# Routed experts in 32-row parts on four column groups of TensorE, in an order made on the chip, with a weight ring of two instead of three

## What is computed

```python
def _swiglu(x, w_gu, w_down):
    g, up = jnp.split(x @ w_gu, 2, axis=-1)
    return (jax.nn.silu(g) * up) @ w_down

def _moe(u, router_w, router_b, exp_w_gu, exp_w_down, shared_w_gu, shared_w_down):
    scores = jax.nn.sigmoid((u @ router_w).astype(jnp.float32))
    _, idx = lax.top_k(scores + router_b.astype(jnp.float32), TOP_K)      # 8 of 128 experts
    s_sel = jnp.take_along_axis(scores, idx, axis=-1)
    wts = s_sel / jnp.sum(s_sel, axis=-1, keepdims=True) * ROUTED_SCALE
    routed = ...   # for each token the weighted sum of _swiglu of its 8 experts
    return routed + _swiglu(u, shared_w_gu, shared_w_down)

# reference(), one layer, 512 tokens of 1024 features, all float32:
#   h = x + g1 * mixer(norm(x))     (a gated recurrence and a gated linear attention)
#   h = h + g2 * moe(norm(h))       out = norm(h)
```

## Time and profile before

| | us |
|---|---|
| runs, median (lowest to highest) | 1280.92 (1279.49 to 1283.02) |
| the profiled execution, its own time | 1282.25 |
| its span | 1280.4 |
| first gate and up product starts | 597.44 |
| last down product ends (starts at 1210.49, runs 3.60) | 1214.09 |
| PE busy over the span | 1216.9 |

### The profile page before, as it was taken

The page is one execution under the profiler, slowest core; times in us unless marked ns, Lnnn a source line. Parts: engine busy times, 40 slices in busy tenths (PEclk is TensorE's granted clock), DMA queues, the critical chain, the costliest instruction groups (busy, mean ns, idle before and its releaser), DMA issues.

```text
span 1280.4 us, 21371 instructions
## 1 busy us (share of the span) xinstructions
PE 1216.9 (95%) x5960; PEld 702.8 (55%) x5961; DVE 603.5 (47%) x1080; ACT 468.4 (37%) x573; POOL 249.4 (19%) x297
## 2 busy tenths in 40 slices
PE   5899999999999999989978999999999999999985
PEld 5678887877888878754323333333343333333332
DVE  4542456659445587763423343423324343234227
ACT  5581225564324232321333334234334343334201
POOL 1000000000000000031433343432434343334200
PEclk9799999999999999989989899999999999999987
DMA  9532203213554674428999996984998989766295
GB/s 335 166 106 82 75 17 115 68 66 132 180 166 145 221 266 154 170 91 318 416 374 369 359 394 260 390 333 152 388 382 305 384 323 390 275 215 255 81 385 239
DMA packets 83842, 305.37 MB, mean 238 GB/s; under 512 B 12627, under 2 KB 15931, under 8 KB 60889
## 3 DMA queue, kind: packets, MB, share of 16 engines
q1 hardware_dynamic: 64120, 261.86, 55.2%
q0 software_dynamic: 14752, 34.48, 7.1%
q10 hardware_dynamic: 4928, 8.49, 1.9%
HBM read 293.92 MB, written 29.89 MB: 253 GB/s over the span
## 4 chain that ended last, share of the span: by engine, by line
PE 82%; DMA 9%; DVE 4%; issue 2%; ACT 2%; SPq 1%; POOL 1%; POOLq 0%; PEld 0%; ACTq 0%; DVEq 0%; PEldq 0%
PE psum L1524 32%; PE psum L1747 23%; PE psum L1794 11%; DMA stage<-in_exp_w_gu 4%; PE psum L1732 3%; PE psum L1497 2%; DMA stage<-in_exp_w_down 2%; PE psum L1817 2%; PE psum L1808 1%; PE psum L1626 1%; DMA xg<-u_rows,row_idx 1%; PE psum L1557 1%; DMA ring<-in_ada_w 1%; PE psum L1671 1%; PE psum L1782 1%
## 5 line engine op out<-in xcount | busy, mean ns | idle before, releaser
L1747 PE MATMUL psum<-w_now,xT 128*64 128x512 f32 x1600 | 362.1, 606 | 16.1 <-DVE w_now L1395 16.0
L1747 PEld LDWEIGHTS psum<-w_now,xT 128*64 128x64 f32 x1600 | 110.3, 140 | 225.7 <-issue 206.8
L1794 PE MATMUL psum<-w_now,mask 128*64 128x512 f32 x784 | 176.4, 592 | 0.0
L671 POOL COPY w_now<-stage 128x2048 f32 x52 | 98.8, 1911 | 252.3 <-issue 209.1
L1524 PE MATMUL psum<-uT_hi,w_hi 128*128 128x512 f32 x352 | 139.3, 396 | 1.1 <-DVE w_lo L444 1.1
L1524 PE MATMUL psum<-uT_hi,w_lo 128*128 128x512 f32 x352 | 137.0, 389 | 0.0
L1524 PE MATMUL psum<-uT_lo,w_hi 128*128 128x512 f32 x352 | 137.0, 389 | 0.0
L444 DVE TENSOR_TENSOR w_lo<-ring,w_hi 128x1024 fp32r<-128x1024 f32 x80 | 94.5, 1221 | 87.1 <-ACT w_hi L437 85.3
L939 ACT ACTIVATE w_now<-stage 128x2048 f32 x52 | 98.7, 1910 | 78.9 <-DMA stage<-in_exp_w_gu 56.7
L437 ACT ACTIVATE w_hi<-ring 128x1024 fp32r<-128x1024 f32 x80 | 82.7, 1056 | 118.0 <-PE psum L1524 59.6
L946 ACT ACTIVATE sel<-psum 128x256 f32<-128x256 f32 x50 | 19.2, 384 | 268.9 <-PE psum L1747 268.9
(11 more groups left out here) (284 smaller groups left out, 1606.2 us busy)
## 6 DMA issues: line engine op xcount, KB each, us to landing
stage<-in_exp_w_gu SPq DMA_DIRECT2D x104, 1024.0 KB, 8.5
stage<-in_exp_w_down SPq DMA_DIRECT2D x52, 1024.0 KB, 8.2
ring<-in_w_in SPq DMA_DIRECT2D x56, 512.0 KB, 5.1
ring<-in_ada_w SPq DMA_DIRECT2D x32, 512.0 KB, 4.7
slots<-expert_rows SPq DMA_DIRECT2D x16, 1024.0 KB, 15.6
ring<-in_ada_w SPq DMA_DIRECT2D x4, 1024.0 KB, 13.3
scale_w<-in_ada_w SPq DMA_DIRECT2D x4, 1024.0 KB, 14.5
ring<-in_w_branch_b SPq DMA_DIRECT2D x8, 512.0 KB, 5.7
```

The source lines that it names most:

```text
L671: pool.tensor_copy(w_now[:, q, 4:6], staged(turn, 4, 2)).then_inc(dn_moved, 1)
L1747: mm = pe.matmul(moe_bank(GU)[at, :], xT[:, s % 2, k, at], gu_part(q, k), start=(k == 0), stop=(k == KT - 1))
L1794: mm = pe.matmul(moe_bank(Y0 + g)[at, :], hT[:, j, at], dn_part(q, j, g), start=(j == 0), stop=(j == 1))
```

## The change

The rows of an expert are cut into parts of 32, and a step handles four parts, one in each group of 32 columns (`STREAMS` = 4). Parts are dealt in turn: part p goes to step p // 4 and stream p % 4. So a large expert sits in all four streams, its consecutive parts side by side, and its weights are copied into up to four places of `w_now`. The experts' order is made on the chip: they are ranked by their count, and taken largest, smallest, second largest, second smallest and so on. `w_now` doubles to four places, and to make room the ring has two places (`STAGES = 6 - STREAMS`), the residual rows are written to DRAM (`h_dram`) ahead of the routed loop and read back (`h_back`) ahead of the tail, and the gathered rows use other buffers. The first weights too now go through the ring; they can be loaded once the order is known. Tables carry two streams per word (`turns_of`).

```diff
-STREAMS = 2
+STREAMS = 4
 W = P // STREAMS
...
-STAGES = 3
+STAGES = 6 - STREAMS
+PAIRS = STREAMS // 2
...
+        def turns_of(eng, n):
+
+            turns = []
+            for j in range(PAIRS):
+                word = eng.value_load(turn_words[0:1, bass.ds(PAIRS * n + j, 1)], min_val=0, max_val=256 * E + E)
+                turns += [word % 256, word // 256]
+            return turns
...
+            for t in range(TT):
+                sp.wait_ge(h_res, TT + t + 1)
+                sp.dma_start(h_dram.rearrange("(t p) d -> p t d", p=P)[:, t], x_tok[:, t]).then_inc(h_out, 16)
+
+            sp.wait_ge(loads_ready, 1)
+            n_loads = sp.value_load(load_count[0:1, 0:1], min_val=TOP_K, max_val=E)
+
+            def load(l, free=None):
+
+                e = sp.value_load(load_expert[0:1, bass.ds(l, 1)], min_val=0, max_val=E - 1)
+                if free is not None:
+                    freed = sp.value_load(load_free[0:1, bass.ds(free, 1)], min_val=1, max_val=TABLE)
                 for g in range(2):
...
+                    if not isinstance(l, int) or l:
+                        sp.wait_ge(gu_in[g], l * 16)
+                    if free is not None:
+                        sp.wait_ge(gu_moved[g], freed)
+                    sp.dma_start(staged(l, 2 * g, 2).rearrange("p a n -> p (a n)"), gu_half(e, g)).then_inc(gu_in[g], 16)
+                if not isinstance(l, int) or l:
+                    sp.wait_ge(dn_in, l * 16)
+                if free is not None:
+                    sp.wait_ge(dn_moved, freed)
+                sp.dma_start(staged(l, 4, 2).rearrange("p a n -> p (a n)"), dn_whole(e)).then_inc(dn_in, 16)
+
+            for l in range(STAGES):
+                load(l)
             sp.wait_ge(tables_ready, 1)
...
+                        with sp.If(n_loads > j + STAGES):
+                            load(j + STAGES, j)
...
+            def move_down(n, qs=range(STREAMS)):
+
+                if not isinstance(n, int) or n:
+                    pool.wait_ge(y_psum, n + 3)
+                turns = turns_of(pool, n)
+                for q in qs:
+                    with pool.If(turns[q] > 0):
+                        pool.wait_ge(dn_in, turns[q] * 16)
+                        pool.tensor_copy(w_now[:, q, 4:6], staged(turns[q] + STAGES - 1, 4, 2)).then_inc(dn_moved, 1)
...
+                turns = turns_of(dve, n)
+                for q in qs:
+                    with dve.If(turns[q] > 0):
+                        dve.wait_ge(gu_in[0], turns[q] * 16)
+                        dve.tensor_copy(w_now[:, q, 0:2], staged(turns[q] + STAGES - 1, 0, 2)).then_inc(gu_moved[0], 1)
...
+            own(stt(key_col, rank_col, -2.0, spare_col, ALU.mult, ALU.add))
+            own.settle()
+            own(stt(key_col, rank_col, 2.0, key_col, ALU.mult, ALU.min))
+            own.settle()
+            ts(load_b, iota_row[:], key_col, 1.0, ALU.subtract, ALU.is_equal).then_inc(key_ready, 1)
+            ts(upto_b, iota_row[:], key_col, 0.0, ALU.subtract, ALU.is_gt).then_inc(key_ready, 1)
...
+            move_first(0, (2, 3))
             shared_up(1)
+            dve.wait_ge(h_out, 16 * TT)
+            move_first(0, (0, 1))
             gated_up(0)
             move_first(1)
...
-            def gate_up(n, s, loads):
+            def gate_up(n, s, copies):
...
-                        pe.wait_ge(gu_moved[g], loads + STAGES)
+                    pe.wait_ge(gu_moved[g], copies)
...
```

More of the change, by code:

```diff
@@ L109, in plan @@
     jobs += [(("out", 1, 3), "dve")] + turned(2) + turned(3)
[L110 removed]
+    jobs += [("router", "act"), ("count", "dve"), ("rank", "dve"), ("loads", "dve"), ("pos", "dve"), ("bstart_col", "dve"), ("bstart_row", "dve"), ("table", "dve")]
     jobs += [(("sgu", m), ("act", "dve")[m % 2]) for m in range(4)]
@@ new lines, in _ @@
+            own.settle()
+            stt(key_row, bank("rank")[:, 0:P], 2.0, spare_row, ALU.mult, ALU.min).then_inc(dve_emptied, 1)
+            wait_emptied(dve, "rank")
+            ts(before_b, key_row, key_col, None, ALU.is_gt).then_inc(order_ready, 1)
+            wait_job(dve, "loads")
+            own(dve.memset(load_expert[:, E:E + STAGES].bitcast(F32), 0.0))
+            own(dve.tensor_copy(load_expert[:, 0:E], bank("loads")[0:1, 0:E]))
+            dve.tensor_copy(load_free, bank("loads")[0:1, E:2 * E]).then_inc(dve_emptied, 1)
@@ L1314, in _ @@
+            own.settle()
+            wait_emptied(dve, "loads")
+            dve.nop().then_inc(loads_ready, 1)
             own(dve.tensor_reduce(w_sum[:], w_left, AX_X, ALU.add))
@@ L1697, in _ @@
             pe.wait_ge(mask_ready, 1)
-            product("count", lambda t: mask_b[:, t], lambda t: ones_b[:, 0:1], dst=bank("count")[:, 0:1], tiles=TT)
+            start_job("count")
+            for t in range(TT):
+                pe.matmul(bank("count")[:, 0:1], mask_b[:, t], ones_b[:, 0:1], start=(t == 0), stop=(t == TT - 1))
+            for t in range(TT):
+                mm = pe.matmul(bank("count")[:, P:2 * P], ones_b[:], mask_b[:, t], start=(t == 0), stop=(t == TT - 1))
+            end_job(mm)
+            pe.wait_ge(less_ready, 1)
+            product("rank", lambda k: ones_b[:], lambda k: less_b, dst=bank("rank")[:, 0:P], tiles=1)
+            shared_product(0, range(5, 6))
+            pe.wait_ge(key_ready, 2)
+            start_job("loads")
+            pe.matmul(bank("loads")[0:1, 0:E], id_cols[:, 0:1], load_b, start=True, stop=True)
+            end_job(pe.matmul(bank("loads")[0:1, E:2 * E], id_cols[:, 2:3], upto_b, start=True, stop=True))
             start_job("pos")
@@ L1787, in _ @@
                 pe.wait_ge(hT_ready, b + 1)
-                pe.wait_ge(dn_moved, loads + STAGES)
+                pe.wait_ge(dn_moved, copies)
                 pe.wait_ge(y_ready, b + 2)
```

284 lines of the change are left out of this document (146 added, 138 removed).

## The result

The changed kernel takes 1496.39 us (median of 4 runs, 1494.56 to 1498.93); the kernel before, beside it, 1281.97 us (4 runs, 1279.49 to 1284.44). The ratio is 1.167, 95% interval 1.165 to 1.170. The profiled execution has a span of 1495.1 us against 1280.4.

A forecast was written before the change was run, and what follows sets the result against it. PE's chain of waits was taken as the bound, with DMA no bound on average. A loop of 787 us against 616.65 (+170), start +9 and tail 0 took 1282.25 to 1460 us, range 1330 to 1575.

The forecast's parts named there:

- ten with two new loads: Loop steps up to 29 where the second load is issued only after the first has landed; 20 us each.
- nine with four copies: Loop steps with four weight copies per engine, one POOL copy ahead of DVE's last; 15.3 us plus 1.9 of clock, 17.2.
- eleven others: Loop steps with three or fewer copies; 12.2 us and 2 for loads and clock, 14.2 each.
- eight rounds: Steps 30 to 34 and 36 to 38, a whole round through the two-place ring between gate and up products; 30.1 us each.
- the early case: Loop steps with two new loads, if they do not wait for loads; 15.3 us.
- the late one: Loop steps with two new loads, if both landings are waited for in turn; 23 us, 26 with the longest landing.
- The rival that bytes or bandwidth set the time: Rival stated for the SP reordering: late steps need more loads than DMA brings, loop within 20 us of 785; no chance given.
- The rival of groups that do not run together: Products take 10.7 us more per step with two column groups at a time; time near 1770 us, chance 0.08.
- Start: Ahead of the first gate and up: two more copies per engine after the last shared product; +9 us, between 4 and 14.
- Tail: Behind the loop: the extra 2 MB written and read back lie beside other work; put at 0.
- The faster rival: Loads in the loop are hidden and only copies count; loop 555 us, kernel 1229 us, chance 0.07.
- The rival of half waits: Loop waits for loads are half those priced, rounds of 22 and two-load steps of 16; time near 1355 us, chance 0.12.

The follow-up runs named there:

- mended order: SP sends a load's down transfer behind the next load's gate and up transfers; changed kernel 1400.68 us, kernel before 1277.4 us, kernel before with two places 1301.69 us.
- quarters: Changed kernel with SP's down transfer behind the next gate and up, each column group walking its own quarter of the list; 1431.34 us, with loop spans of 8 steps 1374.52.
- second dealt run: Changed kernel with SP's down transfer behind the next gate and up, and loop spans of 8 steps in place of 16; 1373.78 us, loop 689.0.
- two kernels with spans of eight: Changed kernel with down transfers behind the next gate and up and 8-step loop spans, once with a list quarter per column group (1374.52 us), once with dealt parts (1373.78).
- with spans of eight: Changed kernel with the loop over steps grouped in spans of 8 instead of 16; 1474.88 us, time behind the loop 67.7 us instead of 89.1.

## Why the prediction held, and where its terms did not

The profiled time was predicted at 1460 us and is 1496.86. The loop was 2 us under its forecast, the start 14.6 and the tail 22.8 over theirs. What the prediction named as its signs is there: 1280 down instructions, 131 copies, 7.07 us for 64 instructions, and in the loop a DMA share of 0.64 and a clock of 0.85.

**The loop: 787 predicted, 785.0 measured.** The classes of steps, taken from the starts of the gate and up products:

| steps | predicted, us each | measured |
|---|---|---|
| ten with two new loads | 20 | 20.2 |
| nine with four copies | 17.2 | 17.0 |
| eleven others | 14.2 | 14.8 |
| eight rounds (30 to 34, 36 to 38) | 30.1 | 28.9 (26.1 to 33.2) |
| last two | 12 | 13.4 |

The eight rounds are where the prediction put them, and step 35, which it left out of them, took 17.7 us. The 20 us of the steps with two new loads is right as a mean only: up to step 12 they take 13.5 to 17.8 us, near the early case (15.3), and after it 21.1 to 25.3, near the late one (23). One of them owes its length to something else. In step 14, 21.1 us under both orders of SP, the chain goes through no landing, but through two stretches in which DVE waits for nothing that the profile shows (the "issue" rows below); the prediction had no such term. That such classes add up to 785 is partly luck.

```profile
816.75 4.27 issue
...
823.40 2.60 issue
```

**Within a round the sum was right and its terms were not.** In the round shown, landing was 5.0 us, not 8.5, and DVE's copy 1.2, not 4.2, since POOL had finished; this is 6.5 less. But POOL made three copies before SP could go on, not 1.5, and they took 6.2 us, not 2.8:

```profile
1222.57 8.03 POOL L703 COPY w_now<-stage 128x2048 f32 x4 [6.88 <-issue]
```

The first of these four ran from 1222.57 to 1225.09, 2.52 us in place of 1.88, as DVE's last copy ran until 1223.34; the third ended at 1228.76. POOL began 1.8 us after the down product, not 1.1 (so in all eight rounds), as it reads two words for the four streams first (line 485); and SP took 2.8 us from POOL's copy to its transfer, not 1.0, as it sends the down transfer and reads two table values in between. Those are 5.9 more. Over the eight rounds POOL made 1.9 copies on average ahead of SP's transfer, and their number orders the rounds: with one copy they took 26.1 to 26.3 us, with two 28.5, with three 28.8 to 32.1; one more, with one copy but a second landing to wait for, took 33.2. So the copies were priced somewhat too low, the table reading on POOL and SP (2.5 us) was left out, and a landing priced 3.5 us too long hid both. The path of the round was right; that its sum was right is luck.

**The cause.** The prediction held that the down transfer's wait for POOL stands ahead of the next expert's weights in one queue. The experiment that changes only this took 102 us of the 168.4 away (95.7 by the medians), all of it from the steps where the prediction has loads waiting. The rival that bytes or bandwidth set the time is refuted with it for this part. The loop in us, under the old and the mended order of SP:

| kernel | old | mended |
|---|---|---|
| before, three places | 616.65 | 610.8 |
| before, two places | 689.1 | 633.9 |
| four groups, quarters | - | 672.3 |
| four groups, dealt (the change) | 785.0 | 682.9 |

The effects do not simply add: the mended order is worth 5.8 us with three places, 55.2 with two, and 102.1 with two and four dealt groups. Down the mended column the ring costs 23.1, four groups 38.4, dealing 10.6 (17 by the second dealt run, 689.0; the medians of the two kernels with spans of eight, 1374.52 and 1373.78, do not differ, as the start comes 7 us later with quarters). 40 steps of more experts each do not run faster than 49 steps of fewer: each gate and up product still waits 3.2 us on average for a copy (with quarters 145.4 us in all, 21.1 of them before the first). How much of the 38.4 is the crowding of new experts and how much the clock, granted at 0.92 against 0.97 over the whole kernel, these runs do not separate. A ring of three under four groups was not tried, since the change gives the third place up for the larger `w_now`.

**Column groups.** Full concurrency was taken from the pair of the earlier trace rows, and the trace confirms it: 7.07 us for 64. The rival of groups that do not run together is out. "TensorE: Matmul & The Clock Gate" of the Trainium skill gives a ratio of 2.38 for three column tiles (Part 3, measured speedup); the loss that it would mean here does not show with four groups in float32.

**Start: +9 predicted, +23.6 measured; this term was mis-sized.** The longer tables moved the shared products' end from 597.4 to 605.0, the 7 us that were priced. Then came 16 us to the first product, where only 2.4 to 3.8 us of copies were expected. 4.8 of them are POOL's copies beside DVE's, by the experiment that moved them. The prediction had this exclusion in its step of four copies and did not apply it to step 0. The others are order on DVE: its first two copies stand behind the index reading and the masks for step 4 (606.13 to 609.56), which wait for PE's last `find`, though PE has nothing left to run then. This last was read from the timeline and not tested.

**Tail: 0 predicted, +22.8 measured; this step failed.** The prediction looked at the extra transfers and not at how the loop is left. 49 steps end one into a span of 16 and have 15 dead steps, 40 leave eight; yet DVE's first sum came 16 us after the last down product before, when the rows it reads had landed, and 48.5 us after it in the changed kernel. The chain of waits shows what passing dead steps holds:

```profile
1421.38 4.89 issue
1426.34 0.07 DVEq L503
1426.41 6.20 issue
1432.61 0.13 DVEq L503
1432.77 0.06 DVEq L510
1432.82 4.76 issue
```

DVE's branches (line 503 is the loop over groups of four steps, line 510 the branch over one dead step) are followed by some 5 us in which it runs nothing; between 1406.2 and 1453.9 there are nine such gaps, 45.7 us together. The queues' view of 1406 to 1454 (packets, MB, share) has packets of instructions in this stretch:

```profile
q14 instruction: 12, 0.10, 0.6%
```

Each of the nine gaps has one or two of these twelve in it, and with spans of eight there are three between 1408 and 1431, and the 21 us are gone. So the gaps are most likely fetches of instructions; that is an inference from the packets, and no run changes only that. Nor is it shown why eight dead steps cost so much here and 15 nothing visible before: the body of the loop is longer, and DMA was busy with other reads in both (share 0.84 from 1406 to 1454, 0.87 from 1214 to 1230 before).

**Odds.** The faster rival needed loads to be hidden; a mean step of 19.4 us (785.0 less the last 10.5, over 40) is far above its break-even of 14.9. The rival of half waits gave 682 for the loop. The changed kernel is nowhere near it, and it is, by chance, what the mended order reaches.

## What to carry to other kernels

Where one in-order queue feeds a ring, ask for each transfer whose copy it waits for and what stands behind it: the answer was worth 102 us in the changed kernel, 55 in the kernel before with two places and 6 with three, at the same bytes. Before a ring gives up a place for wider concurrency, follow the order of the loads through it step by step; averages (DMA share, busy time) showed nothing. And when the number of iterations changes, look at how the unrolled loop is left: dead iterations are not free.

## What the runs showed of the hardware that was not expected

- Four column groups of 32 with 512 moving columns in float32 take 7.07 us for 64 instructions, where two groups of 64 take 7.06 for 32.
- Two DVE copies of 128 x 2048 took 4.64 and 5.14 us beside POOL's copies of the same shape, 2.36 and 2.35 without; ACT's, 3.71 for two, did not change.
- In the changed kernel DVE stands still for some 5 us behind most branches over dead steps (nine gaps of 2.0 to 7.4 us for eight dead steps), with twelve packets of q14 in the gaps. In the kernel before it passed 15 dead steps and was at its first sum 16 us after the last down product.
- Reading tables takes time on a queue: POOL's first copy comes 1.8 us after the down product with two words to read, 1.1 before, with one word to read ahead of it, and SP needs 2.8 us from POOL's copy to its next gate and up transfer (1228.76 to 1231.55).
